# A decoder block's query projection, with the tokens stationary instead of the weights

## Chip, core and metric

One core of a Trainium2 chip. The metric is the device time of one execution in microseconds (us), lower is better. Three executions of the kernel before took 1489.03 to 1489.21 us, with a median of 1489.17 us.

## What is computed

A decoder block on 256 tokens of width 2048, all in f32: a mixer, cross-attention into 256 memory tokens with four heads of width 512, and a gated ConvFFN. The change is in the cross-attention:

```python
def cross_attend(xn, memn, wq, wk, wv, wo):
    q = (xn @ wq).reshape(B, S, XA_HEADS, XA_HEAD_DIM)
    k = (memn @ wk).reshape(B, M, XA_HEADS, XA_HEAD_DIM)
    v = (memn @ wv).reshape(B, M, XA_HEADS, XA_HEAD_DIM)
    scores = jnp.einsum('bshd,bmhd->bhsm', q, k).astype(jnp.float32) * (XA_HEAD_DIM ** -0.5)
    p = jax.nn.softmax(scores, axis=-1).astype(v.dtype)
    o = jnp.einsum('bhsm,bmhd->bshd', p, v).reshape(B, S, XA_HEADS * XA_HEAD_DIM)
    return o @ wo
```

## The kernel before

All weights come as one stream of chunks of 128 x 2048 numbers; a chunk is two panels of 128x1024. Each f32 number is split into a high and a low part (fp32r), and a product is made of three: high by high, high by low, low by high. The split of a panel is one ACT copy (`whi<-raw`, L583) and one DVE subtraction (`wlo<-raw,whi`, L981) that waits for it. Four panel buffers hold two chunks. On ACT and on DVE the program goes chunk by chunk through `step(m, pr, do0, do1, do2)`: it first waits until PE has used both panels of a chunk (`panels_used`), then does `do0`, splits the first panel of the chunk two further on, does `do1`, splits the second panel, does `do2`. Each engine works its own list strictly in the order written, so that list is the whole schedule: what stands in `do0` is ahead of both splits, and nothing of a step starts before PE is through with its chunk.

There are two ways to multiply by a chunk. `narrow` keeps 128 weight columns stationary and streams the tokens (512 columns for `whi`, 256 for `wlo`); one chunk gives 128 output features for all tokens, features on the partitions. `wide` keeps 128 tokens stationary and streams 512 weight columns; a chunk is four k-tiles by 512 features, four chunks make 512 features for all tokens, with tokens on the partitions, in two banks of PSUM. The FFN's up product is wide; its rows are copied out (L887), turned by DVE in blocks of 32x32 (L1414) and the blocks are moved to their partitions by ACT, 16 moves of 32x256 (L894).

The query stage has 16 chunks, four a head, all narrow. A head's q is four times: ACT copies a half (`hl`, L598), DVE adds (L999), ACT and DVE split it (L848, L1389). The attention work of a head stands inside the product of the next head: `scores` (24 matmuls) in chunk 0 after 10 of its 16 k-tiles, `probs_tr` (4 transposes, L498, wait on `pn_ready`) in chunk 1 after 12, `attend` (24 matmuls) in chunk 2 after 10. For the fourth head the three stand in chunks 0, 1 and 2 of the output product (L282 with mixT), which is wide. On DVE and ACT the softmax stands as `do1` of the step of the head's last chunk: DVE's maximum (L1349, L1350) waits for `sc_done`, ACT's two exponentials (L833) for `nb_ready`, then comes the second panel's split on both, and `softmax_norm` (L1355, L1357) as `do2` on DVE. `norm_tr(3)` (8 transposes, L343) of the RMS norm ahead stands in the first chunk.

## Time and profile before

| | |
|---|---|
| median of 3 runs | 1489.17 us |
| the profiled execution | 1489.79 us |
| its span | 1488.0 us |
| PE busy | 1478.4 us (99%), 7186 matmuls |
| PE weight loads | 1247.9 us |
| DVE busy | 1025.6 us (69%) |
| ACT busy | 963.5 us (65%) |
| DMA | 288.93 MB, mean 194 GB/s |

Busy time of PE counts each matmul up to its modelled end, and matmuls overlap, so the distance from one start to the next is what a matmul costs. A few matmul records are missing from the trace, so counts inside a stretch of PE can be low by some per cent while its starts and ends hold.

### The profile page before, as it was taken

The page shows a single profiled execution, that of the slowest core. Times are in us where ns is not written, and L with a number is a line of the kernel's source. Part 1 is how long each engine was busy: PE and PEld are TensorE (multiplying, and loading weights), DVE is VectorE, ACT ScalarE, POOL GpSimd, SP SyncE. Part 2 cuts the span into 40 slices and gives each one's busy share as a digit, 9 for nine tenths or more (in the row PEclk, how much of TensorE's full clock was granted, in tenths as well). Part 3 has the DMA queues.
Part 4 walks back from the last instruction along what each step waited for, and adds up shares of the span by engine and source line. Part 5 has one row for each costly group of instructions (what it writes and reads, how often), then busy time and mean ns, then how long its engine had stood idle before and what let it go on. Part 6 is the DMA issues. An engine that isn't in the chain of part 4 may idle for free.

```text
span 1488.0 us, 22342 instructions
## 1 busy us (share of the span) xinstructions
PE 1478.4 (99%) x7186; PEld 1247.9 (84%) x7186; DVE 1025.6 (69%) x1384; ACT 963.5 (65%) x1477; POOL 2.9 (0%) x9
## 2 busy tenths in 40 slices
PE   9999999999999999999999999999999999999997
PEld 8888888888888888888888888888888888888886
DVE  5756666788888566664665776675857676685696
ACT  6644578745555486554767868586766858576974
POOL 0000000000000000000000000000000000000000
PEclk9999999999999999999999999999999999999999
DMA  9756655565556654445555565556555555656554
GB/s 346 259 193 210 218 180 187 199 200 169 175 175 228 197 184 156 156 153 194 190 184 195 186 201 191 190 188 199 187 197 200 186 194 186 199 188 193 195 197 143
DMA packets 81038, 288.93 MB, mean 194 GB/s; under 512 B 9008, under 2 KB 10544, under 8 KB 80096
## 3 DMA queue, kind: packets, MB, share of 16 engines
q1 hardware_dynamic: 76752, 275.68, 55.8%
q10 hardware_dynamic: 3744, 9.30, 1.8%
q0 software_dynamic: 496, 3.34, 0.6%
q8 instruction: 28, 0.46, 0.1%
q14 instruction: 18, 0.15, 0.0%
HBM read 286.19 MB, written 2.10 MB: 194 GB/s over the span
## 4 chain that ended last, share of the span: by engine, by line
PE 98%; ACT 1%; DVE 0%; issue 0%; DMA 0%; ACTq 0%; DVEq 0%
PE ps L282 98%; ACT whi L583 0%; PE ps L343 0%; DMA hl<-in_first_in 0%; DVE wlo L981 0%; PE ps L444 0%; ACT scr L833 0%; DVE sm_ L1349 0%; PE ps L498 0%; DVE tmp L999 0%; ACT scr L956 0%; ACT vm L971 0%; DVE xres L1499 0%; ACTq L118 0%; ACT whi L624 0%
## 5 line engine op out<-in xcount | busy, mean ns | idle before, releaser
L981 DVE TENSOR_TENSOR wlo<-raw,whi 128x1024 fp32r<-128x1024 f32 x516 | 624.7, 1220 | 314.6 <-ACT whi L583 305.6
L583 ACT ACTIVATE whi<-raw 128x1024 fp32r<-128x1024 f32 x516 | 531.4, 1053 | 222.6 <-PE ps L282 216.2
L282 PE MATMUL ps<-whi,xT 128*128 128x512 f32 x1536 | 475.1, 389 | 0.0
L282 PE MATMUL ps<-whi,mixT 128*128 128x512 f32 x1472 | 457.0, 390 | 0.3 <-ACT whi L624 0.3
L282 PEld LDWEIGHTS ps<-whi,xT 128*128 128x128 f32 x1536 | 288.4, 188 | 59.8
L282 PEld LDWEIGHTS ps<-whi,mixT 128*128 128x128 f32 x1472 | 276.8, 188 | 57.9 <-issue 0.6
L282 PE MATMUL ps<-xT,whi 128*128 128x512 f32 x896 | 310.5, 398 | 0.3
L282 PE MATMUL ps<-wlo,xT 128*128 128x512 f32 x768 | 298.8, 389 | 0.0
L282 PE MATMUL ps<-wlo,mixT 128*128 128x512 f32 x736 | 285.1, 389 | 0.0
L282 PE MATMUL ps<-xT,wlo 128*128 128x256 f32 x896 | 234.9, 278 | 0.0
L282 PEld LDWEIGHTS ps<-xT,whi 128*128 128x128 f32 x896 | 162.8, 188 | 32.2 <-DVE wlo L981 0.9
L282 PEld LDWEIGHTS ps<-xT,wlo 128*128 128x128 f32 x896 | 168.4, 188 | 7.8
L282 PEld LDWEIGHTS ps<-wlo,xT 128*128 128x128 f32 x768 | 144.2, 188 | 29.8
L282 PEld LDWEIGHTS ps<-wlo,mixT 128*128 128x128 f32 x736 | 138.3, 188 | 28.5
L894 ACT ACTIVATE kT<-kT 32x256 f32<-32x256 f32 x352 | 145.9, 414 | 8.0
L598 ACT ACTIVATE hl<-ps 128x256 f32<-128x256 f32 x72 | 27.6, 384 | 112.5 <-PE ps L282 112.4
L1422 DVE SCALAR_TENSOR_TENSOR vm<-kT,par,vm 128x255 f32<-128x255 f32 (+1 forms) x176 | 84.6, 481 | 9.3 <-DVE vm L1422 0.2
L282 PE MATMUL ps<-mixT,whi 128*128 128x512 f32 x256 | 88.7, 393 | 0.0
L999 DVE TENSOR_TENSOR tmp<-ps,hl 128x256 f32<-128x256 f32 x72 | 30.4, 422 | 62.5 <-ACT hl L598 61.8
L282 PE MATMUL ps<-mixT,wlo 128*128 128x256 f32 x256 | 70.6, 277 | 0.0
L1469 DVE TENSOR_TENSOR xres<-ps,xres 128x512 f32<-128x512 f32 x84 | 54.0, 684 | 7.0 <-PE ps L282 6.0
L282 PEld LDWEIGHTS ps<-mixT,whi 128*128 128x128 f32 x256 | 47.9, 188 | 11.0
(186 smaller groups left out, 744.7 us busy)
## 6 DMA issues: line engine op xcount, KB each, us to landing
raw<-in_stream SPq DMA_DIRECT2D x518, 512.0 KB, 3.3
xres<-in_xin ACTq DMA_DIRECT2D x2, 1024.0 KB, 7.3
scr<-in_xt_in ACTq DMA_DIRECT2D x8, 256.0 KB, 3.6
xres<-in_xin POOLq DMA_DIRECT2D x1, 2048.0 KB, 11.9
out_x<-vm SPq DMA_DIRECT2D x8, 256.0 KB, 3.1
raw<-in_stream SPq DMA_DIRECT2D x4, 256.0 KB, 4.3
kT<-in_memt_in ACTq DMA_DIRECT2D x2, 512.0 KB, 5.7
vbuf<-in_memin ACTq DMA_DIRECT2D x1, 1024.0 KB, 10.0
```

The lines of the kernel that those rows point to most:

```text
L282: return nc.tensor.matmul(o, l, r, start=start, stop=stop, skip_group_check=True)
L583: A(whi[:, 2 * pr + s, :], raw[:, 2 * pr + s, :], ACT.Copy).then_inc(hi_done, 1)
L598: A(hl[:, pr, :], ps[:, 4 + pr, T:], ACT.Copy).then_inc(hl_copied, 1)
L894: A(turned[half][q * 32:(q + 1) * 32].rearrange("p j (t i b) -> p j t i b", t=TT, i=4)[:, :, :, i, :], blocks[i * 32:(i + 1) * 32, q], ACT ...
L981: V.tensor_tensor(wlo[:, 2 * pr + s, :], raw[:, 2 * pr + s, :], f32(whi[:, 2 * pr + s, :]), ALU.subtract).then_inc(lo_done, 1)
L999: return V.tensor_tensor(dst, ps[:, 4 + pr, :T], hl[:, pr, :], ALU.add)
L1422: ins = V.scalar_tensor_tensor(out=conv[half][:, k, sh:], in0=turned[half][:, k, :T - sh], scalar=par[:, ds(4 * (8 * g + (2 * k + half)) + ...
L1469: V.tensor_tensor(x, ps[:, 2 * (n % 2) + tt, :], x, ALU.add).then_inc(fin_added, 1)
```

## The change

The query product becomes wide. Head h's four chunks go over the k-tiles 0-3, 4-7, 8-11 and 12-15 and add up in two banks (4 and 5 for heads 0 and 2, 0 and 1 for head 1, 2 and 3 for head 3); the order of `xa_wq` in the stream follows. In the step of the fourth chunk ACT copies the two banks out (`keep_query`), DVE turns them (`turn_query`), and the 16 block moves are shared: ACT does 8, DVE does 8, four behind each split. One ACT copy and one DVE subtraction of 128x1024 (`query_hi`, `query_lo`), in `do0` of the next step, split q. The buffers `q_rows` and `q_blocks` lie in the last quarter of mixT. The narrow product's copies, sums and splits of q go. The attention of a head moves: scores into the middle of chunk 2 of the next head's product, the transposes into the middle of chunk 3, `attend` into the middle of chunk 0 one head later. Behind the fourth head they stand in chunks 2, 3 and 4 of the output product, and `attend` of the third head in chunk 0. The loops over heads are written out.


```diff
         whi = sb("whi", [P, 4, PAN], F32R)
         wlo = sb("wlo", [P, 4, PAN], F32R)
         xT = sb("xT", [P, KT, 2, T], F32R)
+        with ExitStack() as lent:
+            lent.enter_context(nc.sbuf_tensor("mix_low", [P, 12, 2, T], F32))
+            q_rows = lent.enter_context(nc.sbuf_tensor("q_rows", [P, TT, XD], F32))
+            q_blocks = lent.enter_context(nc.sbuf_tensor("q_blocks", [P, 4, 4, TT, 32], F32))
         mixT = sb("mixT", [P, KT, 2, T], F32R)
         kT = sb("kT", [P, KT, T])
         vm = sb("vm", [P, TT, D])
...
         first_mem = hl[:].rearrange("p a b -> p (a b)")[:, :KT + T]
         row_mem = csr[:, 0, :]
         zout = vm
+        Q_BANKS = (4, 0, 4, 2)
         rows_of = kT[:, 0:4, :].rearrange("p (t h) c -> p t (h c)", t=TT)
...
         def stage(g, tt):
             return xres[:, tt, (g % 4) * CG:(g % 4 + 1) * CG]
+
+        def q_move(i, q):
+            return (tmp[q * 32:(q + 1) * 32, 0:4, :].rearrange("p j (t i b) -> p j t i b", t=TT, i=4)[:, :, :, i, :],
+                    q_blocks[i * 32:(i + 1) * 32, q])
         def mem_tile(f):
             return kT[:, f, :] if f else first_mem[:, KT:]
...
                     mid = (lambda: norm_tr(2)) if n == 7 and half else None
                     wide(C_OP // 2 + 4 * half + n // 2, n % 2, mixT, range(k0, k0 + 4), 2 * g, kp == 0, kp == 3, mid)
-            NEXT = {6: lambda: norm_tr(3), 8: lambda: wait_for(nt_lo, 12), 12: lambda: wait_for(nt_lo, 14),
-                    14: lambda: wait_for(nt_lo, KT)}
-
-
             def scores(h1):
                 pe.wait_ge(k_ready, h1)
-                pe.wait_ge(qT_ready, 4 * h1)
+                pe.wait_ge(qT_ready, h1)
                 for tt in range(TT):
                     o, t = bankA[:, tt * T:(tt + 1) * T], slice(tt * P, (tt + 1) * P)
                     for f in range(4):
...
                         last = mm(o, v_lo, p_head[:, 0, mt, :], False, mt == 1)
                 last.then_inc(pv_done, 1)
-            ATT = (scores, probs_tr, attend)
-            pe.wait_ge(nt_lo, 8)
-            for j in range(4):
-                narrow(C_Q // 2 + j // 2, j % 2, xT, {} if j else NEXT, 0 if j else 8)
-            with pe.Fori(1, XH) as h:
-                for j in range(4):
-                    narrow(C_Q // 2 + 2 * h + j // 2, j % 2, xT, {(10, 12, 10)[j]: lambda: [ATT[j](h), 3][1]} if j < 3 else {})
+            for h in range(XH):
+                for n in range(4):
+                    mid = None
+                    if h == 0:
+                        pe.wait_ge(nt_lo, 4 * n + 4)
+                        mid = (lambda: norm_tr(3)) if n == 0 else None
+                    elif n == 0 and h > 1:
+                        mid = lambda: attend(h - 1)
+                    elif n > 1:
+                        mid = lambda: (scores, probs_tr)[n - 2](h)
+                    wide(C_Q // 2 + 2 * h + n // 2, n % 2, xT, range(4 * n, 4 * n + 4), Q_BANKS[h], n == 0, n == 3, mid)
             for half in range(2):
                 for n, (g, kp) in enumerate(WIDE_ORDER):
                     if half == 0:
                         pe.wait_ge(ot_lo, 2 * kp + 2)
                     mid = None
-                    if half == 0 and n < 3:
-                        mid = lambda f=ATT[n]: f(XH)
+                    if half == 0 and n == 0:
+                        mid = lambda: attend(XH - 1)
+                    elif half == 0 and 2 <= n < 5:
+                        mid = lambda: (scores, probs_tr, attend)[n - 2](XH)
                     elif n == 7 and half:
                         mid = lambda: norm_tr(6)
                     wide(C_XO // 2 + 4 * half + n // 2, n % 2, mixT, range(4 * kp, 4 * kp + 4), 2 * g, kp == 0, kp == 3, mid)
...
                 act.wait_ge(stage_moved, 16 * (2 * (g // 4) + g % 2) + 16)
                 hi_tiles(st_turned[g % 2][:, 2 * b:2 * b + 2, :], xT, gain, (4 * g + 2 * b) % KT, nt_hi)
-            def wide_norm(c0, g0, gain, extra, extra2={}):
+            def wide_norm(c0, g0, gain, extra, extra2={}, extra0={}):
                 m, g1 = c0 // 2, g0 + 1
                 for n in range(6):
-                    step(m + n // 2, n % 2, None, extra.get(n), extra2.get(n))
+                    step(m + n // 2, n % 2, extra0.get(n), extra.get(n), extra2.get(n))
                 step(m + 3, 0, None, None, lambda: stage_squares(g0))
                 step(m + 3, 1, None, None, lambda: stage_squares(g1))
                 step(m + 4, 0, None, lambda: move_stage(g0, 0), lambda: move_stage(g0, 1))
...
             def keys_hi(h):
                 A(k_head[:, 0], kT[:, ds(4 * h, 4), :], ACT.Copy).then_inc(k_hi_done, 1)
-            def query_hi(h, j):
-                act.wait_ge(q_sum, 4 * h + (j + 1))
-                A(q_hi[:, j, :], tmp[:, j, :], ACT.Copy).then_inc(q_hi_done, 1)
+            def keep_query(h):
+                for tt in range(TT):
+                    A(q_rows[:, tt, :], ps[:, Q_BANKS[h] + tt, :], ACT.Copy).then_inc(q_kept, 1)
+
+            def move_query(h, i):
+
+                act.wait_ge(q_turned, 2 * h + 2)
+                for q in range(4):
+                    A(*q_move(i, q), ACT.Copy).then_inc(q_moved_act, 1)
+
+            def query_hi(h):
+                act.wait_ge(q_moved_act, 8 * h + 8)
+                act.wait_ge(q_moved_dve, 8 * h + 8)
+                A(q_hi[:], tmp[:, 0:4, :], ACT.Copy).then_inc(q_hi_done, 1)
             def out_parts(h1):
                 act.wait_ge(pv_done, h1)
                 for b in range(2):
                     A(mixT[:, ds(4 * h1 + (2 * b - 4), 2), 0, :], two((bankA, bankB)[b]), ACT.Copy).then_inc(ot_hi, 1)
-            def q_head(h, tail):
+            def last_probs_and_rows(h):
+                if h:
+                    probs_hi(h)
+                keep_query(h)
+
+            def scaled_exps(h):
+                exps(h - 1)
+                if h < XH:
+                    act.wait_ge(sc_done, h)
+                    keys_hi(h)
+
+            def out_and_query(h):
+                if h > 1:
+                    out_parts(h - 1)
+                query_hi(h - 1)
+
+            for h in range(XH):
                 m = C_Q // 2 + 2 * h
-
-                def take(j):
-                    copy_hl(j % 2)
-                    query_hi(h, j)
-
-                def values():
-                    take_values(h)
-                    probs_hi(h)
-
-                def keys():
-                    if tail:
-                        act.wait_ge(sc_done, h)
-                    else:
-                        act.wait_ge(lru_lo, LB)
-                    keys_hi(h)
-
-                step(m, 0, lambda: take(0), None, values if tail else None)
-                step(m, 1, lambda: take(1), keys)
-                step(m + 1, 0, lambda: take(2), (lambda: out_parts(h)) if tail else None)
-                step(m + 1, 1, lambda: take(3), lambda: exps(h))
-
-            q_head(0, False)
-            with act.Fori(1, XH) as h:
-                q_head(h, True)
-            wide_norm(C_XO, 4, O_G3, {2: lambda: out_parts(XH)}, {0: lambda: (take_values(XH), probs_hi(XH))})
+                step(m, 0, (lambda: out_and_query(h)) if h else None)
+                step(m, 1, None, (lambda: take_values(h)) if h else None)
+                step(m + 1, 0, (lambda: scaled_exps(h)) if h else lambda: keys_hi(0))
+                step(m + 1, 1, lambda: last_probs_and_rows(h), lambda: move_query(h, 0), lambda: move_query(h, 1))
+            wide_norm(C_XO, 4, O_G3, {1: lambda: take_values(XH)}, {4: lambda: out_parts(XH)},
+                      {0: lambda: out_and_query(XH), 2: lambda: scaled_exps(XH), 3: lambda: probs_hi(XH)})
             def keep_rows(half):
...
                 dve.wait_ge(nt_hi, 4 * g + 2 * b + 2)
                 lo_tiles(st_turned[g % 2][:, 2 * b:2 * b + 2, :], xT, gain, (4 * g + 2 * b) % KT, nt_lo)
-            def wide_norm(c0, g0, gain, extra1, extra2):
+            def wide_norm(c0, g0, gain, extra1, extra2, extra0={}):
                 m, g1 = c0 // 2, g0 + 1
                 for n in range(6):
-                    step(m + n // 2, n % 2, None, extra1.get(n), extra2.get(n))
+                    step(m + n // 2, n % 2, extra0.get(n), extra1.get(n), extra2.get(n))
                 step(m + 3, 0, lambda: add_stage(g0), None, lambda: turn_stage(g0))
                 step(m + 3, 1, lambda: add_stage(g1))
                 step(m + 4, 0)
...
                 dve.wait_ge(k_hi_done, h + 1)
                 V.tensor_tensor(k_head[:, 1], kT[:, ds(4 * h, 4), :], f32(k_head[:, 0]), ALU.subtract).then_inc(k_ready, 1)
-            def attend_parts(h1):
-                values_lo(h1)
-                probs_lo(h1)
-
             def out_split(h1):
                 for b in range(2):
                     dve.wait_ge(ot_hi, 2 * h1 - 1 + b)
...
                     V.tensor_tensor(mixT[:, k, 1, :], two((bankA, bankB)[b]), f32(mixT[:, k, 0, :]),
                                     ALU.subtract).then_inc(ot_lo, 1)
-            def q_head(h, tail):
-                m, w = C_Q // 2 + 2 * h, W_Q + 4 * h
-
-                def q(j):
-                    narrow_sum(w + j, j % 2, tmp[:, j, :]).then_inc(q_sum, 1)
-                    dve.wait_ge(q_hi_done, 4 * h + (j + 1))
-                    V.tensor_tensor(q_lo[:, j, :], tmp[:, j, :], f32(q_hi[:, j, :]), ALU.subtract).then_inc(qT_ready, 1)
-
-                step(m, 0, lambda: q(0), None if tail else q_scale, (lambda: attend_parts(h)) if tail else None)
-                step(m, 1, lambda: q(1), None, lambda: keys_lo(h))
-                step(m + 1, 0, lambda: q(2), (lambda: out_split(h)) if tail else None)
-                step(m + 1, 1, lambda: q(3), lambda: softmax_max(h), lambda: softmax_norm(h))
-
-            q_head(0, False)
-            ch.enter(0, 2, 1)
-            with dve.Fori(1, XH) as h:
-                ch.reg = h
-                q_head(h, True)
-            ch.leave(XH)
-            wide_norm(C_XO, 4, O_G3, {0: lambda: attend_parts(XH), 2: lambda: out_split(XH)}, {})
+            def turn_query(h):
+                dve.wait_ge(q_kept, 2 * h + 2)
+                if h:
+                    dve.wait_ge(q_moved_act, 8 * h)
+                for tt in range(TT):
+                    V.transpose(q_blocks.rearrange("p q j t b -> p t j q b")[:, tt], q_rows[:, tt, :]).then_inc(q_turned, 1)
+
+            def move_query(h, i):
+                dve.wait_ge(q_turned, 2 * h + 2)
+                for q in range(4):
+                    V.tensor_copy(*q_move(i, q)).then_inc(q_moved_dve, 1)
+
+            def query_lo(h):
+                dve.wait_ge(q_hi_done, h + 1)
+                V.tensor_tensor(q_lo[:], tmp[:, 0:4, :], f32(q_hi[:]), ALU.subtract).then_inc(qT_ready, 1)
+
+            def probs_and_blocks(h):
+                if h:
+                    probs_lo(h)
+                turn_query(h)
+
+            def out_and_query(h):
+                if h > 1:
+                    out_split(h - 1)
+                query_lo(h - 1)
+
+            def norm_and_keys(h):
+                softmax_norm(h - 1)
+                if h < XH:
+                    keys_lo(h)
+
+            for h in range(XH):
+                m = C_Q // 2 + 2 * h
+                step(m, 0, (lambda: out_and_query(h)) if h else q_scale)
+                step(m, 1, None, (lambda: values_lo(h)) if h else None)
+                step(m + 1, 0, (lambda: softmax_max(h - 1)) if h else None, (lambda: norm_and_keys(h)) if h else lambda: keys_lo(0))
+                step(m + 1, 1, lambda: probs_and_blocks(h), lambda: move_query(h, 2), lambda: move_query(h, 3))
+            wide_norm(C_XO, 4, O_G3, {1: lambda: values_lo(XH), 2: lambda: norm_and_keys(XH), 4: lambda: out_split(XH)}, {},
+                      {0: lambda: out_and_query(XH), 2: lambda: softmax_max(XH - 1), 3: lambda: probs_lo(XH)})
             dve.wait_ge(stage_squared, 16)
             ch.link(V.tensor_reduce(sm_[:, 3, :], ssum[:, :, 0:4], AX_X, ALU.add))
             mean_of(sm_[:, 3, :])
...
         ffn += [gate[:, n], up[:, n]] + ([down[n - 1]] if 0 < n < NG - 2 else [])
     ffn += [down[n] for n in range(NG - 3, NG)]
     parts = [wide_stream(a["xa_wv"][0], order=VM_ORDER), narrow_chunks(a["xa_wk"][0]), yu, wide_stream(v), heads,
-             wide_stream(a["w_out"][0], (2, 3, 0, 1)), narrow_chunks(a["xa_wq"][0]), wide_stream(a["xa_wo"][0])] + ffn
+             wide_stream(a["w_out"][0], (2, 3, 0, 1)), wide_chunks(a["xa_wq"][0]).swapaxes(0, 1).reshape(16, P, D), wide_stream(a["xa_wo"][0])] + ffn
     s = np.concatenate(parts)
     assert s.shape[0] == NC
     return np.ascontiguousarray(s.reshape(NC, P, 2, PAN).transpose(0, 2, 1, 3)).reshape(2 * NC, P, PAN)
...
```

ACT around the first head's exponentials, each instruction with its waits; `whi<-raw` is a panel's high part. Before:

```order
L583 ACTIVATE whi<-raw 128x1024 [waits panels_used,raw_landed2]
L833 ACT_TABLE_LOAD
L833 ACTIVATE scr,sm_<-ps,sm_ 128x256 [waits nb_ready]
L833 ACTIVATE scr,sm_<-ps,sm_ 128x256
L583 ACTIVATE whi<-raw 128x1024 [waits panels_used,raw_landed3]
```

After:

```order
L596 ACTIVATE whi<-raw 128x1024 [waits panels_used,raw_landed3]
L846 ACT_TABLE_LOAD [waits nb_ready]
L846 ACTIVATE scr,sm_<-ps,sm_ 128x256 [waits panels_used]
L846 ACTIVATE scr,sm_<-ps,sm_ 128x256
L857 ACTIVATE k_head<-kT 128x1024 [waits sc_done]
L596 ACTIVATE whi<-raw 128x1024 [waits panels_used,raw_landed0]
L596 ACTIVATE whi<-raw 128x1024 [waits panels_used,raw_landed1]
```

The exponentials moved from between the two splits of a step to ahead of both, the copy of the keys came in between, and the table load now waits for the maximum.

DVE at the same place; the maximum is the TENSOR_REDUCE, the normalisation the RECIPROCAL and the two TENSOR_SCALAR. Before:

```order
L981 TENSOR_TENSOR wlo<-raw,whi 128x1024 [waits hi_done]
L1349 TENSOR_REDUCE sm_<-ps 128x2 [waits sc_done]
L1350 TENSOR_TENSOR sm_<-sm_ 128x2 [waits chain_v]
L981 TENSOR_TENSOR wlo<-raw,whi 128x1024 [waits hi_done]
L1355 RECIPROCAL sm_<-sm_ 128x2 [waits p_ready]
L1357 TENSOR_SCALAR scr<-scr,sm_ 128x256 [waits chain_v]
L1357 TENSOR_SCALAR scr<-scr,sm_ 128x256
```

After:

```order
L1370 TENSOR_REDUCE sm_<-ps 128x2 [waits sc_done,panels_used]
L1371 TENSOR_TENSOR sm_<-sm_ 128x2 [waits chain_v]
L1002 TENSOR_TENSOR wlo<-raw,whi 128x1024 [waits hi_done]
L1376 RECIPROCAL sm_<-sm_ 128x2 [waits p_ready]
L1378 TENSOR_SCALAR scr<-scr,sm_ 128x256 [waits chain_v]
L1378 TENSOR_SCALAR scr<-scr,sm_ 128x256
L1391 TENSOR_TENSOR k_head<-kT,k_head 128x1024 [waits k_hi_done]
L1002 TENSOR_TENSOR wlo<-raw,whi 128x1024 [waits hi_done]
```

The maximum now waits for the end of the chunk that holds the scores (`panels_used`) as well as for the scores; a split stands between maximum and normalisation in both.

PE up to the transposes of the probabilities (ident,scr), which stand in the second panel of chunk 1 before and between the panels of chunk 3 after. Before:

```order
L282 MATMUL ps<-xT,whi 128x512 [waits lo_done]
L282 MATMUL ps<-xT,wlo 128x256
L282 MATMUL ps<-xT,whi 128x512
L282 MATMUL ps<-xT,wlo 128x256
L282 MATMUL ps<-xT,whi 128x512
L282 MATMUL ps<-xT,wlo 128x256
L282 MATMUL ps<-xT,whi 128x512
L282 MATMUL ps<-xT,wlo 128x256
L498 MATMUL ps<-ident,scr 128x128 [waits pn_ready]
L498 MATMUL ps<-ident,scr 128x128 x3
```

After:

```order
L293 MATMUL ps<-whi,xT 128x512 [waits lo_done]
L293 MATMUL ps<-wlo,xT 128x512
L293 MATMUL ps<-whi,xT 128x512 x2
L293 MATMUL ps<-wlo,xT 128x512
L293 MATMUL ps<-whi,xT 128x512 x2
L293 MATMUL ps<-wlo,xT 128x512
L293 MATMUL ps<-whi,xT 128x512 x2
L293 MATMUL ps<-wlo,xT 128x512
L293 MATMUL ps<-whi,xT 128x512
L505 MATMUL ps<-ident,scr 128x128 [waits pn_ready]
L505 MATMUL ps<-ident,scr 128x128 x3
```

Before, 6 k-tiles of chunk 0 and 12 of chunk 1 stand between the scores and the transposes; after, two panels of 12 wide matmuls, of which the second is shown.

## Rows read from the trace of the kernel before

**Rows 1.** The page: the chain that ended last, by engine.
```profile
...
PE 98%; ACT 1%; DVE 0%; issue 0%; DMA 0%; ACTq 0%; DVEq 0%
...
```

**Rows 2.** Timeline of PE, both ends of the query stage: start us, us, engine, operation, count.
```profile
556.87 0.61 PE L282 MATMUL ps<-xT,whi 128*128 128x512 f32 x2
...
558.95 1.05 PE L343 MATMUL ps<-ident,xres 128*128 128x128 f32 x8
559.75 0.71 PE L282 MATMUL ps<-xT,whi 128*128 128x512 f32 x2
...
666.48 0.40 PE L282 MATMUL ps<-whi,mixT 128*128 128x512 f32 x1
```

**Rows 3.** Timeline of PE: two starts a narrow chunk apart, two a wide chunk apart.
```profile
575.11 0.40 PE L282 MATMUL ps<-xT,whi 128*128 128x512 f32 x1
...
580.66 0.40 PE L282 MATMUL ps<-xT,whi 128*128 128x512 f32 x1
...
920.55 0.62 PE L282 MATMUL ps<-whi,mixT 128*128 128x512 f32 x2
...
925.99 0.62 PE L282 MATMUL ps<-whi,mixT 128*128 128x512 f32 x2
```

**Rows 4.** Timeline of PE: a head's values, a head's scores, what follows each.
```profile
598.23 3.03 PE L282 MATMUL ps<-p_head,v_heads 128*128 128x256 f32 x24
601.09 0.63 PE L282 MATMUL ps<-xT,whi 128*128 128x512 f32 x2
...
612.21 0.39 PE L282 MATMUL ps<-k_head,q_hi 128*128 128x256 f32 x2
...
615.07 0.63 PE L282 MATMUL ps<-xT,whi 128*128 128x512 f32 x2
```

**Rows 5.** Timeline of DVE behind the scores of one head, idle time ahead in brackets.
```profile
615.27 0.69 DVE L1349 TENSOR_REDUCE sm_<-ps 128x2 f32<-128x512 f32 x1 [2.82 <-PE ps L282]
...
618.37 1.23 DVE L981 TENSOR_TENSOR wlo<-raw,whi 128x1024 fp32r<-128x1024 f32 x1 [2.22 <-ACT whi L583]
...
619.71 0.62 DVE L1357 TENSOR_SCALAR scr<-scr,sm_ 128x256 f32<-128x256 f32 x2
```

**Rows 6.** Timeline of ACT: keys and split; the split behind the exponentials.
```profile
599.04 1.04 ACT L844 ACTIVATE k_head<-kT 128x1024 fp32r x1
599.99 1.04 ACT L583 ACTIVATE whi<-raw 128x1024 fp32r<-128x1024 f32 x1
...
617.29 1.05 ACT L583 ACTIVATE whi<-raw 128x1024 fp32r<-128x1024 f32 x1
```

**Rows 7.** Timeline of ACT around two loads of a function table.
```profile
563.50 1.28 ACT L602 ACT_TABLE_LOAD   x1
564.79 0.20 ACT L602 ACTIVATE sm_<-sm_ 128x2 f32<-128x2 f32 x1
...
582.49 1.28 ACT L833 ACT_TABLE_LOAD   x1
```

**Rows 8.** Timelines: ACT from PSUM; DVE's turn and ACT's moves, FFN.
```profile
605.54 1.06 ACT L853 ACTIVATE mixT<-ps 128x512 f32 x2
...
917.57 1.30 DVE L1414 STREAM_TRANSPOSE kT<-kT 128x512 f32<-128x512 f32 x2
...
920.74 1.72 ACT L894 ACTIVATE kT<-kT 32x256 f32<-32x256 f32 x4
```

**Rows 9.** Timeline of PE's opening; windows: busy by engine (PE first), then clock.
```profile
1.00 4.21 PE L282 MATMUL ps<-ones 128*128 128x128 f32 x18 [1.00 <-POOL ones L268]
5.50 1.95 PE L282 MATMUL ps<-whi,mixT 128*128 128x512 f32 x4 [0.29 <-ACT whi L624]
7.29 0.62 PE L282 MATMUL ps<-wlo,mixT 128*128 128x512 f32 x2
...
1480.00:1488.00 8.00, 0.00 (x0) 0.00 (x0) 3.00 (x7) 2.71 (x7) 0.00 (x0) 0.82 0.71 230
```

More of the change, by code:

```diff
@@ L207, in build @@
                              "pv_done", "ot_hi", "ot_lo"))
-        q_sum, q_hi_done, k_hi_done, k_ready, p_hi_done, v_hi_done = (
-            sem(n) for n in ("q_sum", "q_hi_done", "k_hi_done", "k_ready", "p_hi_done", "v_hi_done"))
+        q_kept, q_turned, q_moved_act, q_moved_dve = (
+            sem(n) for n in ("q_kept", "q_turned", "q_moved_act", "q_moved_dve"))
+        q_hi_done, k_hi_done, k_ready, p_hi_done, v_hi_done = (
+            sem(n) for n in ("q_hi_done", "k_hi_done", "k_ready", "p_hi_done", "v_hi_done"))
         rows_kept, blocks_turned, blocks_moved, tap_set, gate_taps, gate_silu, hid4_ready, hid4_hi, down_ready = (
```

## Prediction, made before the run

> **What bounds the kernel now.** I read the page's chain first: PE carries 98% of it [rows 1], so only what changes PE's own matmuls, or makes PE wait, moves the time. Then the timeline of PE over the query stage. It runs from 556.87 to 666.48 us, 109.61 us [rows 2]. Of that the eight transposes of the norm take 559.75 - 558.95 = 0.80 us [rows 2], a head's scores 615.07 - 612.21 = 2.86 and its values 601.09 - 598.23 = 2.86 [rows 4], and its four transposes half of the eight, 0.40. Three heads' attention stands in the stage: 3 x 6.12 = 18.36. The 16 chunks are left with 109.61 - 0.80 - 18.36 = 90.45 us, 5.65 us each. The third view is that of DVE and ACT behind the scores: DVE sat idle 2.82 us until the scores were there [rows 5], so the softmax begins the moment PE gives them, while PE still has six k-tiles of this chunk and twelve of the next ahead of the transposes.
>
> **The product itself.** A narrow chunk costs 580.66 - 575.11 = 5.55 us between two equal places, a wide one in the FFN 925.99 - 920.55 = 5.44 us [rows 3]. Both stream the same columns, so 0.11 us a chunk is all that the form gives: 16 x 0.11 = 1.8 us. The other 90.45 - 16 x 5.55 = 1.65 us are small gaps where a split of a panel comes late behind the four passes of copy, sum and split of q. Many of these passes go, so part of the gaps goes. The gain is between 1.8 and 16 pieces at 5.44, 90.45 - 87.04 = 3.4 us; I take 2.8, nearer to the upper end, since the wide stages with similar side work run at 5.44. A head's 48 small matmuls and 4 transposes and the stream of weights stay as they are; the DMAs are the same in number and size.
>
> **The softmax chain, the main term.** The scores now stand in the middle of chunk 2 and the transposes in the middle of chunk 3. Between them PE has two panels, 5.44 us, hardly less than the 18 k-tiles of before (18 x 5.55 / 16 = 6.24). But the maximum moved into `do0` of chunk 2's step, and a step waits until PE has used its whole chunk. The chain therefore starts one panel later, at the start P of chunk 3, and PE wants its result after one panel, at P + 2.72. The chain, each step as the rows give it: the maximum starts 615.27 - 615.07 = 0.20 after P [rows 4, 5]. ACT's next instruction behind both exponentials starts 617.29 - 615.27 = 2.02 later [rows 5, 6], which makes P + 2.22. There stands the copy of the next keys, worth 599.99 - 599.04 = 0.95 [rows 6]: P + 3.17. ACT's split follows, and DVE's split starts 618.37 - 617.29 = 1.08 behind its start [rows 5, 6]: P + 4.25. The scaling starts 619.71 - 618.37 = 1.34 later and its two instructions take 0.62 [rows 5]: P + 6.21. PE waits 6.21 - 2.72 = 3.5 us. Nothing on PE can fill this, since it takes its matmuls in the written order.
>
> This is the wait of the second and the third head. For the first head the load of the exponentials' function table comes on top: it ran at 582.49, behind a split and ahead of the wait for the maximum [rows 7]; now it waits for the maximum itself, so its 1.28 us [rows 7] lie in the chain: 4.8 us. For the fourth head, in the output product, there are no next keys: 3.5 - 0.95 = 2.55 us. Sum: 4.8 + 3.5 + 3.5 + 2.55 = 14.35 us. When PE goes on, the panels that it needs next have been split while it stood, so none of the four waits brings another; they also don't shorten anything later.
>
> The price of the table load is weighed once against the notes. The row shows 1.28 us and the next activation 0.01 us behind it, 563.50 + 1.28 to 564.79 [rows 7]. The Trainium skill ("ScalarE: Activation LUTs", section "What ACT_TABLE_LOAD costs") counts about 1.28 us for the load and 1.38 us more for a drain at each switch of set. By the page the first wait would be 1.4 us longer; the rows show no such drain, and the sum goes by them.
>
> **The way of q to the scores.** In the step of the fourth chunk, counted from the chunk's end: ACT copies two banks out in 1.06, DVE turns them in 1.30 and ACT's four moves take 1.72 [rows 8]. DVE's four moves of 32x256 have no row. They are bounded from below by two scalings of 128x256 in 0.62 [rows 5], so 1.2 for four, and from above by ACT's 1.72 [rows 8]; I take 1.4, since DVE passes the same 256 elements a partition as in the scaling. ACT: copies to 1.1, split to 2.1, moves (turned at 2.4) to 4.1, split to 5.2, moves to 6.9. DVE: turn to 2.4, split to 3.6, moves to 5.0, split (ACT's at 5.2) to 6.45, moves to 7.85. In the next step, for the first head: ACT's split of q to 8.9 and of the panel to 10.0; DVE's part of q to 10.1 and of the panel to 11.35. PE wants this panel two chunks after, at 10.9, less 0.2 for the end of its last matmul: a wait of about 0.65 us, between 0.2 and 1.3 by the two bounds. For the later heads that chunk holds the values' 2.86 us, and the same sum (copies of the output 1.06, q 1.04, panel 1.05, DVE's two 1.23) ends 0.7 us ahead of PE. The scores themselves find q ready by some 5 us. Cost: 0.65 us.
>
> **Sum.** 14.35 + 0.65 - 2.8 = +12.2 us. On the profiled execution, 1489.79 us (its span of 1488.0 and 1.8 around it), this gives 1502.0; the median of the three runs lies 0.6 lower: 1501.4 us.
>
> **Rivals.** (A) *PE's clock falls in the waits.* Now PE is never idle long enough to show; after, it stands for 4.8, 3.5, 3.5 and 2.55 us. For it: after the start from idle, PE began at 1.00 and the first long matmuls came 1.95 us for four, against 0.62 for two from 7.29 on [rows 9], so some 6.3 us went at 1.2 GHz instead of 2.4, which costs half of it, 3.1 us. Against it: at the end PE is idle from 1480 on and the clock of the last 8 us is 0.82 in the mean [rows 9]; one step to half makes 8 x 0.18 / 0.5 = 2.9 us low and 5.1 us still full, longer than the longest wait here. If only the first wait does it: 1504.5 us. If the three long ones do, 3 x 3.1 = 9.3 more: 1510.7 us. The Trainium skill ("TensorE: Matmul & The Clock Gate", section "Why this matters for your kernels") warns of just this, that idle gaps between bursts of matmuls send the clock back to half; by its rule the first wait at least is in danger, and no stretch of this trace with PE at work shows such a fall.
>
> (B) *The chain is hidden, and the change is not slower.* Should the maximum run as soon as the scores are there, while PE is in chunk 2's second panel, and the table be loaded ahead, the chain would start 2.72 us earlier: 0.8 us are left for each of three heads and nothing for the fourth, 2.4 + 0.65 - 3.4 = -0.3 us, 1488.8 us. It is decided by whether probabilities are ready within 2.72 us of P. Against it stands the order of DVE: the maximum waits for `panels_used` too.
>
> (C) *The blocks are late for every head.* If DVE's moves cost what ACT's do, or the two slow each other, the 0.7 us of slack behind the later heads goes and each has a panel late. That is 1.3 for the first and up to 0.8 for three more: +3, 1504.4 us. For it: both engines work through nearly the whole step. Against it: the FFN makes ACT do twice as many moves and keeps up.
>
> **How the numbers follow.** Forecast 0.71; A 0.17 (0.11 for the first wait alone, 0.06 for more); C 0.07; B 0.03; waits clearly shorter than worked out, for a reason that I don't see, 0.02. The forecast's own bounds are the gain of 1.8 to 3.4, q's 0.2 to 1.3, and 0.3 us on each wait, about 1499.5 to 1503.5. To hold 8 in 10 with the first wait's fall and with C the range goes to 1498.5 to 1505.5. A measurement of this kernel can tell about 0.2%, 3 us, from no change: B alone lies within or below. Faster 0.01, within 0.03, slower 0.96.
>
> **What would show it.** The waits view would have PE waiting for the scaling four times, 4.8 us the longest, some 14 us in all; from one head's scores to the next it is some 4 x 5.44 + 6.1 + 3.5 = 31.4 us; a wide chunk without attention takes 5.44 us; the clock stays full. Wrong would be: no idle of PE ahead of the transposes (B), 0.43 us between long matmuls behind a wait (A), idle of PE at a panel in chunk 2 of every head (C).

## The result and the profile after

| | before | after |
|---|---|---|
| median | 1489.14 us (4 runs) | 1509.99 us (4 runs: 1509.89, 1510.14, 1510.10, 1506.20) |
| profiled execution | 1489.79 us | 1509.89 us |
| its span | 1488.0 us | 1508.1 us |
| ratio | | 1.0133, 95% interval 1.0118 to 1.0147 |

The change made the kernel slower by 1.3%, 20.1 us between the two profiled executions. The forecast had the sign and named a wait of the right size, but 12 us in place of 20; 1510 us lies above its range of 1498.5 to 1505.5.

The page of the kernel after, with PE's granted clock in 40 slices and the chain that ended last, as in [rows 1]:

```profile
...
PEclk9999999999999999889999999999999999999999
...
PE 97%; DVE 1%; ACT 1%; issue 0%; DMA 0%; ACTq 0%; DVEq 0%
...
```

Two slices are no longer full. They lie at 603 to 678 us, in the query stage. The waits view (who waited for what: us in total, times, the longest) has a pair of lines that the kernel before has not:

```profile
PEld ps L505 <- DVE scr L1378: 15.7, 4, 5.1
PE ps L505 <- DVE scr L1378: 14.1, 4, 4.7
```

Timelines of DVE and ACT behind the first head's scores; these are the lines that answer to [rows 5] and [rows 6]:

```profile
599.18 0.69 DVE L1370 TENSOR_REDUCE sm_<-ps 128x2 f32<-128x512 f32 x1 [4.20 <-PE ps L293]
...
604.56 1.23 DVE L1002 TENSOR_TENSOR wlo<-raw,whi 128x1024 fp32r<-128x1024 f32 x1 [4.50 <-ACT whi L596]
...
605.89 0.62 DVE L1378 TENSOR_SCALAR scr<-scr,sm_ 128x256 f32<-128x256 f32 x2
...
600.14 1.28 ACT L846 ACT_TABLE_LOAD   x1 [7.40 <-DVE sm_ L1371]
601.44 0.56 ACT L846 ACTIVATE scr<-ps,sm_ 128x256 f32<-128x256 f32 x1
...
602.53 1.05 ACT L857 ACTIVATE k_head<-kT 128x1024 fp32r<-128x1024 f32 x1
603.48 1.99 ACT L596 ACTIVATE whi<-raw 128x1024 fp32r<-128x1024 f32 x2
```

This is the chain as the prediction walked it. The maximum starts at 599.18; ACT loads the table only then, 1.28 us, then takes the exponentials, the keys and the split; DVE's split is at 604.56 and the scaling at 605.89, done at 606.5. PE at the same place (start, us, count, and in brackets how long it was idle), then the transposes of the other three heads:

```profile
601.47 0.39 PE L293 MATMUL ps<-whi,xT 128*128 128x512 f32 x1
606.57 1.11 PE L505 MATMUL ps<-ident,scr 128*128 128x128 f32 x4 [4.71 <-DVE scr L1378]
607.33 0.78 PE L293 MATMUL ps<-whi,xT 128*128 128x512 f32 x1
607.90 0.63 PE L293 MATMUL ps<-wlo,xT 128*128 128x512 f32 x1
608.33 1.05 PE L293 MATMUL ps<-whi,xT 128*128 128x512 f32 x2
...
612.73 0.40 PE L293 MATMUL ps<-wlo,xT 128*128 128x512 f32 x1
...
641.00 0.90 PE L505 MATMUL ps<-ident,scr 128*128 128x128 f32 x3 [3.43 <-DVE scr L1378]
...
675.27 1.12 PE L505 MATMUL ps<-ident,scr 128*128 128x128 f32 x4 [3.44 <-DVE scr L1378]
...
708.51 0.66 PE L505 MATMUL ps<-ident,scr 128*128 128x128 f32 x4 [2.49 <-DVE scr L1378]
708.92 0.48 PE L293 MATMUL ps<-whi,mixT 128*128 128x512 f32 x1
```

PE's last matmul before the wait starts at 601.47, the transposes at 606.57. Less the 0.23 us that a matmul costs anyway this is 4.87 us. The other three waits are 3.59, 3.60 and 2.65 us by the same count (idle plus 0.16), 14.7 us in all.

The second thing in these lines is new. Behind the first wait the four transposes take 607.33 - 606.57 = 0.76 us, against 708.92 - 708.51 = 0.41 behind the fourth, and 13 matmuls from 607.33 to 612.73 cost 5.40 us, 0.42 each; at 612.73 the step is back at 0.23. That is 5.40 - 13 x 0.227 + 0.35 = 2.8 us lost at half speed. Windows of the same trace (us; busy time by engine, PE first; then the granted clock):

```profile
605.00:613.00 8.00, 6.43 (x19) 5.24 (x20) 3.74 (x6) 0.77 (x2) 0.00 (x0) 0.57 0.41 131
...
639.00:647.00 8.00, 6.00 (x17) 4.92 (x18) 4.18 (x6) 0.91 (x2) 0.00 (x0) 0.57 0.39 131
...
673.00:681.00 8.00, 5.73 (x17) 4.69 (x18) 4.19 (x6) 1.18 (x2) 0.00 (x0) 0.57 0.38 131
```

Three times the clock was low: 0.57 over 8 us is (1 - 0.57) x 8 / 0.5 = 6.9 us at 1.2 in place of 2.4 GHz (6.8 by windows of 1 us, which the text below uses). Each time it began while PE stood at the transposes, and PE worked slowly for the rest of it. The fourth wait, of 2.65 us, had no fall.

The ends of the two stages (query and output product) give the balance; the first two lines are of the kernel after, the last of the kernel before, whose stage began at 556.87 [rows 2]:

```profile
556.05 0.39 PE L293 MATMUL ps<-whi,xT 128*128 128x512 f32 x1
...
780.86 0.39 PE L293 MATMUL ps<-whi,xT 128*128 128x512 f32 x1
...
760.76 0.39 PE L282 MATMUL ps<-whi,xT 128*128 128x512 f32 x1
```

After: 780.86 - 556.05 = 224.81 us. Before: 760.76 - 556.87 = 203.89. So 20.9 us arose here, and 0.8 came back ahead of the stage, where nothing was changed. Of the 20.9, waits at the transposes are 14.7, the wait behind the first head's q is 0.9 (below), three falls are some 8, and the product gives back some 2.6. The last two are settled by experiments.

DVE's moves and splits for the first head's q, and PE at the panel that came late:

```profile
582.54 1.23 DVE L1410 COPY tmp<-q_blocks 32x256 f32<-32x256 f32 x4
...
588.07 1.23 DVE L1414 TENSOR_TENSOR q_lo<-tmp,q_hi 128x1024 fp32r<-128x1024 f32 x1 [1.28 <-ACT q_hi L872]
589.22 1.22 DVE L1002 TENSOR_TENSOR wlo<-raw,whi 128x1024 fp32r<-128x1024 f32 x1
...
590.49 0.50 PE L293 MATMUL ps<-whi,xT 128*128 128x512 f32 x1 [0.74 <-DVE wlo L1002]
```

Four moves on DVE take 1.23 us, near the lower bound of 1.2. DVE's part of q is at 588.07 and the panel's low part at 589.22; PE goes on at 590.49 after 0.74 us idle, 0.9 with the end of the matmul. The prediction had 0.65. The later heads show no such line.

### The profile page after: what moved, and what is told of

The parts are those of the page before. It is cut to its first block, busy times and chain, and to the rows that moved or that the text cites. A ratio compares the mean times of both kernels' runs of the same rounds, so it can differ in the third digit from the quotient of the medians.

```text
span 1508.1 us, 21959 instructions
## 1 busy us (share of the span) xinstructions
PE 1483.9 (98%) x7058; PEld 1246.5 (83%) x7058; DVE 1031.7 (68%) x1396; ACT 974.4 (65%) x1489; POOL 2.9 (0%) x9
## 4 chain that ended last, share of the span: by engine, by line
PE 97%; DVE 1%; ACT 1%; issue 0%; DMA 0%; ACTq 0%; DVEq 0%
PE ps L293 96%; DVE wlo L1002 0%; ACT whi L596 0%; PE ps L505 0%; PE ps L354 0%; DMA hl<-in_first_in 0%; ACT scr L846 0%; ACT k_head L857 0%; DVE scr L1378 0%; DVE sm_ L1370 0%; PE ps L455 0%; DVE q_blocks L1405 0%; ACT tmp L867 0%; DVE q_lo L1414 0%; DVE tmp L1410 0%
## 5 line engine op out<-in xcount | busy, mean ns | idle before, releaser
L293 PE MATMUL ps<-whi,xT 128*128 128x512 f32 x1792 | 561.3, 392 | 0.7 <-DVE wlo L1002 0.7
L293 PEld LDWEIGHTS ps<-whi,xT 128*128 128x128 f32 x1792 | 339.9, 190 | 72.0 <-DVE wlo L1002 1.2
L293 PE MATMUL ps<-wlo,xT 128*128 128x512 f32 x896 | 351.3, 392 | 0.0
L293 PE MATMUL ps<-xT,whi 128*128 128x512 f32 x640 | 222.5, 399 | 0.0
L293 PEld LDWEIGHTS ps<-wlo,xT 128*128 128x128 f32 x896 | 169.9, 190 | 35.1
L293 PE MATMUL ps<-xT,wlo 128*128 128x256 f32 x640 | 168.9, 278 | 0.0
L293 PEld LDWEIGHTS ps<-xT,whi 128*128 128x128 f32 x640 | 117.0, 188 | 23.3
L293 PEld LDWEIGHTS ps<-xT,wlo 128*128 128x128 f32 x640 | 120.3, 188 | 5.0
L611 ACT ACTIVATE hl<-ps 128x256 f32<-128x256 f32 x56 | 21.4, 383 | 97.7 <-PE ps L293 97.6
L1020 DVE TENSOR_TENSOR tmp<-ps,hl 128x256 f32<-128x256 f32 x56 | 23.7, 423 | 60.0 <-ACT hl L611 59.9
```

The lines of the kernel that those rows point to most:

```text
L293: return nc.tensor.matmul(o, l, r, start=start, stop=stop, skip_group_check=True)
L611: A(hl[:, pr, :], ps[:, 4 + pr, T:], ACT.Copy).then_inc(hl_copied, 1)
L1020: return V.tensor_tensor(dst, ps[:, 4 + pr, :T], hl[:, pr, :], ALU.add)
```

## The experiments

Theory 1: the softmax chain starts a panel late, PE waits four times, and the waits let the clock fall. Its rivals: the falls belong to the wide product with its turns and moves (2), the moves and turns cost something themselves (3), the keys aren't in the chain (4), a normalisation ahead of a split makes PE wait for panels (5).

| kernel | median us | ratio to before, 95% | waits at transposes, us | stretches at half clock |
|---|---|---|---|---|
| after | 1509.99 | 1.0133 (1.0118-1.0147) | 4.87, 3.59, 3.60, 2.65 | 3 of 6.8 |
| after_again | 1506.80 | 1.0122 (1.0107-1.0138) | the same | 2 of 3.4 |
| e1_early | 1487.71 | 0.9987 (0.9978-0.9997) | none | none |
| e2_keys_later | 1503.68 | 1.0094 (1.0077-1.0110) | 3.93, 2.65, 2.65, 2.65 | 6.8 and 3.4 |
| e3_keys_table | 1499.95 | 1.0067 (1.0051-1.0084) | 2.65 four times | 1 of 3.4 |
| e4_one_wait | 1494.75 | 1.0034 (1.0022-1.0047) | 4.87 | 1 of 3.4 |
| e5_early_q | 1486.38 | 0.9981 (0.9972-0.9990) | none | none |
| e7_norm_first | 1491.36 | 1.0015 (1.0005-1.0024) | 1.84, 0.57, 0.57, 0.57 | none |
| b1_waits_in_before | 1513.86 | 1.0167 (1.0151-1.0182) | 4.08, 4.09, 4.08, 4.87 | 3 of 3.4, 1 of 6.8 |

The stretches are those of the one profiled execution of each. The kernel before had 1489.14 us in the series of the first row, 1489.38 in that of e1 to e4 and 1489.08 in that of the others.

### e1_early: the softmax starts with the scores

```diff
-                step(m, 1, None, (lambda: take_values(h)) if h else None)
-                step(m + 1, 0, (lambda: scaled_exps(h)) if h else lambda: keys_hi(0))
+                step(m, 1, None, (lambda: take_values(h)) if h else None, (lambda: exps(h - 1)) if h else None)
+                step(m + 1, 0, (lambda: next_keys(h)) if h else lambda: keys_hi(0))
...
-                step(m, 1, None, (lambda: values_lo(h)) if h else None)
-                step(m + 1, 0, (lambda: softmax_max(h - 1)) if h else None, (lambda: norm_and_keys(h)) if h else lambda: keys_lo(0))
+                step(m, 1, None, (lambda: values_lo(h)) if h else None, (lambda: (softmax_max(h - 1), softmax_norm(h - 1))) if h else None)
+                step(m + 1, 0, None, lambda: keys_lo(h))
```

The output product's steps follow in the same way; `next_keys` is the wait for the scores and the copy.

> The changed kernel with the whole softmax of a head (maximum, exponentials, normalisation) moved from the step of chunk 2 to the end of the step of chunk 1, behind its two splits, on ACT and DVE, so that it starts when the scores are there; the keys stay in the step of chunk 2. Theory 1 (the softmax chain starts a panel late, PE waits four times, and the waits let the clock fall): in the changed kernel's trace the four gaps of PE are 4.87 + 3.59 + 3.60 + 2.65 = 14.7 us and three falls cost some 8.4 us. Both go: 1509.9 - 23 = 1487 us, clock full throughout. Rival 2 (the clock falls because of the wide product with its turns and moves, not because of the waits): 14.7 us go and 8.4 stay, 1495 us, clock 0.992. Rival 3 (the block moves and late panels are a cost of their own): over 1490 us with a full clock.

Measured: 1487.71 us, 22.3 below the kernel after and 1.7 below that of before. Timeline of PE at the first head's transposes (no brackets: no idle), of DVE around its softmax, and windows over the two stages with the clock:

```profile
602.32 0.60 PE L505 MATMUL ps<-ident,scr 128*128 128x128 f32 x4
...
594.36 1.22 DVE L1006 TENSOR_TENSOR wlo<-raw,whi 128x1024 fp32r<-128x1024 f32 x1
597.03 0.69 DVE L1374 TENSOR_REDUCE sm_<-ps 128x2 f32<-128x512 f32 x1 [1.45 <-PE ps L293]
...
599.38 0.62 DVE L1382 TENSOR_SCALAR scr<-scr,sm_ 128x256 f32<-128x256 f32 x2
...
556.00:662.00 106.00, 105.26 (x530) 89.14 (x529) 73.60 (x106) 68.62 (x107) 0.00 (x0) 1.00 0.46 159
662.00:760.00 98.00, 98.00 (x473) 82.59 (x472) 60.92 (x78) 65.23 (x111) 0.56 (x1) 1.00 0.53 183
```

DVE's last split starts at 594.36 and is done at 595.58; DVE then waits 1.45 us for the scores; the normalisation is done at 600.0, 2.3 us before PE comes for it. The clock is full. Rivals 2 and 3 fall: turns, moves and the wide form are all still there. The same balance as above gives the worth of the product: the two stages of this kernel take 758.90 - 556.65 = 202.25 us, 1.6 less than before, with the late panel of 0.9 in them; so the product's new form gives 2.5 us.

### e2_keys_later and e3_keys_table: the chain made shorter link by link

```diff
-                step(m + 1, 0, (lambda: scaled_exps(h)) if h else lambda: keys_hi(0))
+                step(m + 1, 0, (lambda: exps(h - 1)) if h else lambda: keys_hi(0), None, (lambda: keys_hi(h)) if h else None)
```

DVE's `keys_lo` moves behind both splits likewise. In e3 one line of ACT's list more, behind the splits of chunk 1's step:

```diff
-                step(m, 1, None, (lambda: take_values(h)) if h else None)
+                step(m, 1, None, (lambda: take_values(h)) if h else None, (lambda: A(lg[:, 1, :], lg[:, 0, :], ACT.Exp)) if h == 1 else None)
```

> The changed kernel with the copy of the next keys (ACT) and its low part (DVE) put behind both splits of the same step; everything else as it is. Theory 1: 0.95 us go from each of the first three waits, which become 3.9, 2.65 and 2.65 us, with the fourth at 2.65; 11.85 us in all. In the changed kernel the clock fell in the three waits of 3.6 us and more and not in that of 2.65 us, so one fall of about 2.9 us is left: 1509.9 - 2.85 - 5.5 = 1501.5 us, or 1498.7 without any fall. Rival 2 (falls belong to the wide product or to any idle time): three falls stay, 1507 us. Rival 4 (the keys' copy isn't in the chain): no change, 1510 us.

> As e2, and an exponential of 128x8 numbers, used by nothing, is put behind the splits of chunk 1's step of the second head, so that the function table is loaded there and not behind the maximum. Theory 1: the first wait loses 1.28 us as well; four waits of 2.65 us, 10.6 us in all, none of them long enough to let the clock fall: 1509.9 - 4.1 - 8.4 = 1497.4 us, clock full. Rival 2: three falls stay, 1505.8 us. If the notes' price of 2.7 us for a switch of table held, the first wait would shrink by 2.7 and the time by 1.4 more.

Measured: 1503.68 and 1499.95 us. The waits went as expected: the keys are worth 0.94 us in each of three heads, so rival 4 falls, and the table 1.28 in the first (3.93 to 2.65 us). Waits and windows of e2:

```profile
PE ps L505 <- DVE scr L1380: 11.2, 4, 3.8
...
604.00:612.00 8.00, 5.85 (x16) 4.76 (x17) 4.19 (x6) 2.00 (x3) 0.00 (x0) 0.57 0.37 131
612.00:639.00 27.00, 25.06 (x133) 21.32 (x131) 17.17 (x26) 17.56 (x28) 0.00 (x0) 1.00 0.35 117
639.00:643.00 4.00, 3.45 (x11) 2.94 (x12) 2.77 (x4) 0.41 (x1) 0.00 (x0) 0.57 0.65 213
643.00:710.00 67.00, 62.01 (x328) 52.91 (x327) 41.80 (x60) 37.47 (x58) 0.56 (x1) 1.00 0.43 145
```

Waits and windows of e3:

```profile
PE ps L505 <- DVE scr L1380: 10.0, 4, 2.5
...
605.00:610.00 5.00, 5.00 (x18) 3.99 (x17) 1.94 (x2) 0.25 (x1) 0.00 (x0) 0.66 0.59 210
610.00:710.00 100.00, 92.52 (x490) 79.03 (x489) 61.74 (x89) 55.18 (x86) 0.56 (x1) 1.00 0.43 147
```

But both times are over theory 1's expectation, by 2.2 and 2.5 us, since it had taken a wait of 2.65 us as too short for a fall. In e2 the second wait, of 2.65 us, was followed by one, and in e3 the first; the others of the same length were not. The theory needed an addition: it isn't the length alone.

### e4_one_wait: one wait, one fall

e1 with the first head left as the change put it; ACT's part of the edit, DVE's maximum and normalisation of the first head likewise:

```diff
+            def next_keys(h):
+                if h == 1:
+                    exps(0)
+                act.wait_ge(sc_done, h)
+                keys_hi(h)
```

> As e1, but the first head's softmax stays where the change put it, with the table load and the keys in its chain; only the second to fourth are early. Theory 1: one wait of 4.87 us is left and one fall of 2.9 us: e1 + 7.8 = about 1494.8 us with one stretch of about 6.8 us at half clock. Without a fall e1 + 4.9 = 1491.9 us. Rival 2: three falls, 1500 us.

Measured: 1494.75 us, e1 and 7.0 us, where the wait is 4.87. Windows over the fall and behind it:

```profile
606.00:611.00 5.00, 4.07 (x13) 3.41 (x14) 3.11 (x6) 0.00 (x0) 0.00 (x0) 0.66 0.45 159
611.00:710.00 99.00, 99.00 (x522) 85.14 (x521) 65.66 (x93) 58.76 (x90) 0.56 (x1) 1.00 0.45 157
```

One fall, shorter than in the kernel after ((1 - 0.66) x 5 / 0.5 = 3.4 us low), worth about 1.7 us by half of its length; with the wait 6.6 of the 7.0 us.

### e7_norm_first: DVE's normalisation ahead of the split

```diff
-                step(m + 1, 0, (lambda: softmax_max(h - 1)) if h else None, (lambda: norm_and_keys(h)) if h else lambda: keys_lo(0))
+                step(m + 1, 0, (lambda: (softmax_max(h - 1), softmax_norm(h - 1))) if h else None, lambda: keys_lo(h))
```

> The changed kernel with one thing altered, DVE's normalisation put ahead of the first panel split of its step instead of behind it; ACT's order stays. Theory 1: the copy of the keys, ACT's split and DVE's split leave the chain. The exponentials are done 2.0 us behind the maximum's start, the normalisation some 0.9 later: a wait of 0.4 us for three heads and 1.7 for the first with its table load, 2.9 us in all in place of 14.7, and no fall of the clock or one of 1.7 us: 1487.7 + 2.9 = 1490.6 us (to 1492.3). Rival 5 (the split delayed by the normalisation makes PE wait for a panel instead): 3 us or more at each of four places, over 1497 us.

Measured: 1491.36 us. The waits view:

```profile
PE ps L505 <- DVE scr L1378: 2.9, 4, 1.7
```

2.9 us of idle where there were 14.1, and no late panel besides the 0.74 us behind the first head's q, which the kernel after has too: rival 5 falls. The late start alone costs little. What made the waits long is what stood between maximum and normalisation, above all the two splits and the keys.

### b1_waits_in_before: the waits without the wide product

The kernel before, with DVE kept busy ahead of the normalisation:

```diff
+                for _ in range(4):
+                    ch.link(V.tensor_tensor(dmask[:], kT[:, 0:4, :], kT[:, 4:8, :], ALU.mult))
                 ch.link(V.reciprocal(sm_[:, 3, :], sm_[:, 7, :]))
...
-            ch.enter(0, 2, 1)
+            ch.enter(0, 6, 1)
```

> The kernel before, with the narrow product, and four multiplications of 128x1024, whose result nothing uses, ahead of DVE's normalisation in each head: 5.0 us of DVE, of which about 1 us (0.3 for the fourth head) is slack. PE then waits some 4.0 us three times and 4.6 us once at the same transposes, 16.6 us. Theory 1 (waits of this length let the clock fall, whatever product stands around them): three or four falls of 2 to 3 us each on top, 1489.3 + 16.6 + 8 = 1514 us, mean clock about 0.992. Rival 2 (the falls belong to the wide product with its turns and moves): clock full, 1506 us.

Measured: 1513.86 us. Waits and windows:

```profile
PE ps L498 <- DVE scr L1359: 16.5, 4, 4.7
...
596.00:600.00 4.00, 3.44 (x12) 3.06 (x13) 2.99 (x6) 3.14 (x4) 0.00 (x0) 0.57 0.00 0
...
630.00:635.00 5.00, 4.33 (x17) 3.86 (x18) 4.00 (x7) 3.94 (x6) 0.00 (x0) 0.66 0.08 8
...
664.00:669.00 5.00, 4.22 (x17) 3.75 (x18) 3.96 (x8) 3.82 (x6) 0.00 (x0) 0.66 0.02 5
...
695.00:703.00 8.00, 4.74 (x15) 3.95 (x16) 7.09 (x9) 0.60 (x1) 0.00 (x0) 0.57 0.21 73
```

Four waits of 4.1 to 4.9 us, 17.1 us in all, and four falls; 1489.1 + 17.1 leaves 7.7 us to them. Around the first three waits the product is the narrow one, and no q is turned or moved anywhere; the fourth wait stands in the output product, which is wide in both kernels. So the falls follow the waits, not the wide product.

### e5_early_q: e1 with q's split between the panels

```diff
-                step(m, 0, (lambda: out_and_query(h)) if h else None)
+                step(m, 0, (lambda: out_parts(h - 1)) if h > 1 else None, (lambda: query_hi(h - 1)) if h else None)
```

DVE likewise.

> e1, and the split of q (one copy on ACT, one subtraction on DVE, 128x1024 each) moved from ahead of both panel splits of its step to between them. Theory 1 (apart from the softmax, the one late panel behind the first head's q is the only wait that the change brings): the 0.9 us gap of PE behind that head goes, and 1487.7 becomes 1486.8 us. Rival 3 (moves and turns cost something that no gap shows): no change, 1487.7 us.

Measured: 1486.38 us against 1489.08 before, the fastest of all: 1.3 us below e1, where 0.9 was expected (the two come from different series, whose kernels before differ by 0.3). PE has no idle left in the two stages, which in this trace take 757.29 - 556.09 = 201.20 us, 2.7 less than before. Rival 3 falls a second time. Against before the median gains 2.7 us too, near the product's 2.8 of the prediction.

### after_again: the changed kernel once more

> The changed kernel itself, for a second trace and more times. Its four times so far are 1509.9, 1510.1, 1510.1 and 1506.2 us. Theory 1, with one addition (whether a wait lets the clock fall and how long it stays low depends on when the wait comes, which differs from execution to execution, not on its length alone): the gaps of PE are the same to 0.05 us, the times are again spread over several us between 1502 (one fall) and 1510 (three), in steps that match the number and length of the stretches at half clock. If length alone decided, all would be within 0.5 us.

Measured: 1505.52, 1508.08, 1508.61 and 1505.53 us, median 1506.80. Waits and windows of the new trace:

```profile
PE ps L505 <- DVE scr L1378: 14.1, 4, 4.7
...
605.00:613.00 8.00, 6.19 (x23) 5.16 (x24) 4.46 (x7) 1.90 (x4) 0.00 (x0) 0.79 0.39 131
...
639.00:647.00 8.00, 6.92 (x26) 5.64 (x27) 4.22 (x8) 1.88 (x4) 0.00 (x0) 0.79 0.40 131
...
673.00:681.00 8.00, 7.60 (x42) 6.65 (x43) 5.82 (x9) 3.69 (x7) 0.00 (x0) 1.00 0.40 133
```

The waits are the same lines as in the first trace, 14.1 us four times over, 4.7 the longest. The clock is not: 0.79 over 8 us twice, 3.4 us low each, and none behind the third wait of 3.6 us. So the same program with the same waits lost about 8 us to the clock in one execution and about 3.4 in the other (the two stages take 220.24 us here and 224.81 there), and its eight times lie between 1505.5 and 1510.1 us. Length alone doesn't decide. Behind the second wait the clock fell at 640.92, 0.84 us after PE had gone on at 640.08; in the first trace it fell 1.3 us before PE went on. What sets the moment wasn't tried, and stays open.

## Why the prediction was wrong

**The product.** Right. 2.8 us were taken, 2.5 to 2.7 measured (e1, e5).

**The softmax chain.** Right, link by link: 4.8, 3.5, 3.5 and 2.55 us were worked out, 4.87, 3.59, 3.60 and 2.65 came. The keys' 0.95 and the table's 1.28 were taken out one after the other (e2, e3) and were worth just that. The table's switch showed no drain: the load at 600.14 takes 1.28 and the exponential follows at 601.44, as [rows 7] had it, and e3 took 1.28 us off the wait, not more. The 1.38 us of drain that the Trainium skill ("ScalarE: Activation LUTs", section "What ACT_TABLE_LOAD costs") adds are not seen here.

**The way of q.** Right in place, 0.65 against 0.9 us; the later heads have no late panel, so rival C did not come. Rival B did not either: the maximum did wait for the chunk's end.

**The clock.** This is the step that failed: the sum put a fall of PE's clock at nothing. The prediction had the mechanism as rival A, with a price of 3.1 us a fall (measured 1.5 to 2.9, half of the low stretch that was left when PE went on) and the time for three falls, 1510.7 us, which is near what came; but it gave more than one fall 0.06, and the range ended below it. That 1510.7 met the median so well is in part luck, since the eight times of this kernel lie between 1505.5 and 1510.1.

The ground for the low chance was [rows 9]: at the end of the kernel before PE is idle and the clock stays full some 5.1 us longer, more than the longest wait. From one stretch it took a length below which nothing happens. The runs show none: falls came behind waits of 2.65 us (e2, e3) and stayed out behind 3.6 us (after_again). The same stretch at the end of other traces would have told otherwise. Windows over it, of the kernel after and of e1, whose last matmuls end at 1500.08 and 1478.13:

```profile
1500.00:1508.00 8.00, 0.07 (x1) 0.00 (x0) 3.01 (x7) 2.82 (x7) 0.00 (x0) 0.70 0.72 235
...
1478.00:1486.00 8.00, 0.12 (x1) 0.00 (x0) 3.00 (x7) 2.87 (x7) 0.00 (x0) 0.65 0.73 237
```

By the sum of rival A the clock was low for 8 x 0.30 / 0.5 = 4.8 us and 5.6 us, so it fell 3.1 and 2.3 us after the last matmul; in the kernel before it was 5.2, in after_again 5.4, and in six of the ten traces under 3.5 us. The 13 falls behind waits came 2.0 to 4.7 us after PE's last matmul, in the same spread. The prediction had one value from the upper end of it and used it as a bound.

The sentence of the Trainium skill ("TensorE: Matmul & The Clock Gate", section "Why this matters for your kernels"), that idle gaps between bursts bring the half clock back, stood beside it, and the traces agree with it in 13 falls behind waits. They also show that a fall need not come: the clock stayed full behind seven waits of 2.65 us and one of 3.6. With the result known, one to four falls at 1.5 to 2.9 us each above 1501.4, some 1503 to 1513 us, would have been the range to give.

**The bounds.** The bounds that the prediction names for its own forecast add up to 1499.2 to 1504.2, a little more than the 1499.5 to 1503.5 that it writes. Nothing hangs on it.

## What to carry to other kernels

When PE is the bound and a change makes it wait some microseconds at a time, add the clock to the price: here 14.7 us of waits cost 18 to 23 us. Ask of every moved step not only when its input is there but which wait its engine sits behind and what stands between its links: here DVE's normalisation moved ahead of one split (e7) took 15 to 19 of the 18 to 21 us back, and the softmax at the end of the step before (e1) all of it, and the wide product then was worth its 2.7 us. One stretch of one trace is no bound on what a clock does: the same stretch gave 2.3 to 5.4 us in ten traces.

## What the runs showed of the hardware

- The clock fell from full to half after 2.65, 3.6, 3.9, 4.1 and 4.9 us of waiting, while PE stood or within 1 us after it had gone on, and stayed full behind 0.6 and 1.8 us (e7) and behind the 0.9 us at the late panel (seven traces). Behind 2.65 us it fell twice and stayed up seven times; behind 3.6 us it fell three times in four, behind 3.9 us and more each of eight times. It was low for 3.4 or 6.8 us, and PE lost half of the part in which it worked: 1.5 to 2.9 us.
- At the end of the kernel the clock fell 2.3 to 5.4 us after the last matmul, in ten traces that end with the same work.
- A DVE copy of 32x256 numbers to other partitions costs 0.31 us (four in 1.23), ACT's 0.43 (four in 1.72 to 1.74).
- The spread of the times is a hint of it and no more: the kernel after, with four waits, lies within 4.6 us (8 executions) and b1 within 2.0 (4); without waits at the transposes e5 lies within 0.4 (11), e1 within 0.8 (10), and the kernel before within 1.3 (21) and 2.1 (15).
